# The third mixer's sixteen chunks: a loop of two bodies against code written out, and the mean of the output against a centring matrix

## What is computed

```python
def step(state, inp):                     # state: heads x 64 (v) x 64 (k)
    r_t, w_t, k_t, v_t, al_t, be_t = inp
    sa = jnp.einsum("bhvk,bhk->bhv", state, al_t)
    state = (state * w_t[:, :, None, :] + sa[..., None] * be_t[:, :, None, :]
             + v_t[..., None] * k_t[:, :, None, :])
    return state, jnp.einsum("bhvk,bhk->bhv", state, r_t)

_, y = lax.scan(step, state0, xs)
mean = jnp.mean(y, axis=-1, keepdims=True)
var = jnp.mean(jnp.square(y - mean), axis=-1, keepdims=True)
y = ((y - mean) * lax.rsqrt(var + RW_GN_EPS)).reshape(bsz, seq, RW_WIDTH) * ln_w + ln_b
bonus = jnp.sum(r * k * r_k, axis=-1, keepdims=True) * v
y = y + bonus.reshape(bsz, seq, RW_WIDTH)
return (y * jax.nn.silu(g)) @ w_out
```

## Time and profile before

| | us |
|---|---|
| median of 3 runs | 3883.31 |
| lowest and highest of them | 3881.01, 3886.58 |
| the profiled execution | 3878.87 |
| its span, first to last instruction | 3877.1 |
| span of the stage of this change, from the first L1725 to the end of the last chunk | about 590 |

### The profile page before, as it was taken

One profiled execution on the slowest core, in us unless ns is written; L12 is line 12 of the kernel. 1 busy time (PEld: TensorE's weight loads), 2 busy tenths in 40 slices (PEclk: granted clock), 3 DMA queues, 4 the chain that ended last, 5 costly groups with the idle time before them and its releaser, 6 DMA issues. The chain is left out here.

```text
span 3877.1 us, 74722 instructions
## 1 busy us (share of the span) xinstructions
PE 3420.5 (88%) x32138; PEld 2120.4 (55%) x32138; DVE 1853.0 (48%) x2539; ACT 1387.1 (36%) x2002; POOL 693.2 (18%) x422
## 2 busy tenths in 40 slices
PE   6978999969798697989998899978799999888889
PEld 3335766644343244888887466645544466545434
DVE  3654566552424533545554456633352366623352
ACT  3553445432454431333333435532211255512111
POOL 2000000020000001333332033322260133132330
PEclk8989999979899798999999999999999999999999
DMA  5101101031243443111111221010012211020121
GB/s 157 33 21 53 39 27 38 22 109 33 76 98 93 105 117 105 42 60 51 51 60 40 66 73 49 7 53 28 14 55 71 60 38 33 1 64 17 41 76 44
DMA packets 308035, 215.19 MB, mean 56 GB/s; under 512 B 125379, under 2 KB 283918, under 8 KB 305166
## 3 DMA queue, kind: packets, MB, share of 16 engines
q1 hardware_dynamic: 307320, 210.70, 18.1%
q10 hardware_dynamic: 442, 0.37, 0.0%
HBM read 173.26 MB, written 41.98 MB: 56 GB/s over the span
## 5 line engine op out<-in xcount | busy, mean ns | idle before, releaser
L140 PE MATMUL psum<-u,w_hi 128*128 128x512 f16 x2816 | 857.0, 387 | 101.9 <-DVEq L796 32.1
L140 PE MATMUL psum<-u,w_lo 128*128 128x512 f16 x1408 | 542.6, 385 | 0.0
L140 PEld LDWEIGHTS psum<-u,w_hi 128*128 128x128 f16 x2816 | 279.6, 100 | 451.4 <-issue 57.5
L97 POOL TENSOR_TENSOR w_hi<-stage,w_scale 128x1024 f16<-128x1024 f32 x76 | 144.9, 1907 | 1157.3 <-PE psum L2258 414.1
L1061 PE MATMUL psum<-w_hi,merged 128*128 128x512 f16 x768 | 235.9, 389 | 25.0 <-PEq L2790 9.1
L2468 DVE CUSTOM_DVE_ANT_0 probs_att<-psum,bias_att 128x1024 f32<-128x1024 f32 x128 | 156.7, 1225 | 168.2 <-PE psum L2280 167.7
L2258 PE MATMUL psum<-u,w_hi 128*128 128x512 f16 x768 | 231.4, 383 | 6.3 <-PEq L964 6.3
L140 PEld LDWEIGHTS psum<-u,w_lo 128*128 128x128 f16 x1408 | 140.0, 99 | 173.2 <-issue 12.5
L1061 PE MATMUL psum<-held_hi_out,merged 128*128 128x512 f16 x768 | 231.0, 379 | 0.0
L115 DVE SCALAR_TENSOR_TENSOR w_lo<-stage,w_hi 128x1024 f16<-128x1024 f32 x100 | 120.0, 1220 | 135.2 <-ACT w_hi L109 135.0
L101 POOL TENSOR_TENSOR w_lo<-stage,w_hi 128x1024 f16<-128x1024 f32 x76 | 177.3, 2333 | 10.8
(11 more groups left out here) (441 smaller groups left out, 6815.4 us busy)
## 6 DMA issues: line engine op xcount, KB each, us to landing
stage<-w_in SPq DMA_DIRECT2D x72, 512.0 KB, 3.8
X<-rwkv_chunks SPq DMA_DIRECT2D x16, 1792.0 KB, 7.6
stage<-ab_w_in SPq DMA_DIRECT2D x48, 512.0 KB, 5.1
rwkv_chunks<-work_rp SPq DMA_DIRECT2D x44, 512.0 KB, 5.6
stage<-rw_w_in SPq DMA_DIRECT2D x32, 512.0 KB, 5.0
stage<-w_out SPq DMA_DIRECT2D x24, 512.0 KB, 5.6
X<-x SPq DMA_DIRECT2D x16, 512.0 KB, 10.9
stage<-ab_w_out SPq DMA_DIRECT2D x16, 512.0 KB, 5.3
```

The lines of the kernel that those rows point to most:

```text
L97: pool.tensor_tensor(K.w_hi[:, slot, :], K.stage[:, slot, :], scale, ALU.mult).then_inc(K.w_half[slot], 1)
L140: last = pe.matmul(K.psum[:, bank, :], w[:, k, :], u[:, k, cols], start=(k == 0 and n == 0), stop=(k == KT - 1 and n == 2))
```

## The change

Two things are done in `rwkv_chunks`. The loop is gone: `chunk_steps` calls the body for each chunk from -1 to 15 with a Python number, so all engines get the 17 bodies one behind the other, and all waits are for constants. `held` is gone too: each of its waits is put on the next instruction, and nothing adds to `seen`. SP's loads are written out in the same way, with the four waits that they had.

And the mean of the output is gone: DVE makes `centre`, the identity less a 64th of `pair_ones`, once ahead of the chunks, and v is turned by a 64x64 block of `centre` where it was turned by the identity. The matmul of the mean on TensorE and the subtraction on DVE are dropped; ACT's square waits for its own copy of the output by a drain, where it waited for `centred`.

```diff
+        centre = sb("centre", [P, P])
-        def held(eng, semaphore, value):
-
-            eng.wait_ge(semaphore, value)
-            eng.sem_inc(seen, 1)
-        def program(eng, body):
-
-            body(-1, 1, True, False, True)
-            body(0, 0, True, True, True)
-            with eng.Fori(0, (RW_N - 4) // 2) as i:
-                body(i * 2 + 1, 1, True, True, True)
-                body(i * 2 + 2, 0, True, True, True)
-            body(RW_N - 3, 1, True, True, True)
-            body(RW_N - 2, 0, True, True, False)
-            body(RW_N - 1, 1, False, True, False)
+        def chunk_steps(body):
+
+            for ch in range(-1, RW_N):
+                body(ch, ch % 2, ch + 1 < RW_N, ch >= 0, ch + 2 < RW_N)
...
-                    sp.dma_start(raw[:, p], A["scratch"][bass.ds(ch, 1)].rearrange("c p a j t -> p (c a) j t")
+                    sp.dma_start(raw[:, p], A["scratch"][ch]
                                  ).then_inc(raw_in[p], 16)
                 load(0, 0)
                 load(1, 1)
-                with sp.Fori(0, (RW_N - 2) // 2) as i:
-                    for p in range(2):
-                        sp.wait_ge(ar_ready, i * 2 + (p + 1))
-                        sp.wait_ge(bk_ready, i * 2 + (p + 1))
-                        sp.wait_ge(turned["v"], i * 2 + (p + 1))
-                        sp.wait_ge(gate_ready, i * 2 + (p + 1))
-                        load(i * 2 + (p + 2), p)
+                for ch in range(2, RW_N):
+                    sp.wait_ge(ar_ready, ch - 1)
+                    sp.wait_ge(bk_ready, ch - 1)
+                    sp.wait_ge(turned["v"], ch - 1)
+                    sp.wait_ge(gate_ready, ch - 1)
+                    load(ch, ch % 2)
...
-                    held(pe, ar_ready, c + 1)
-                    held(pe, bk_ready, c + 1)
+                    pe.wait_ge(ar_ready, c + 1)
+                    pe.wait_ge(bk_ready, c + 1)
...
-                            last = pe.matmul(bank(TURN[n])[hp, j], x[hp, j, :], K.ident[hp, hp], start=True, stop=True)
+                            last = pe.matmul(bank(TURN[n])[hp, j], x[hp, j, :], (centre if n == "v" else K.ident)[hp, hp],
+                                             start=True, stop=True)
...
-                def mean(ch):
-                    held(pe, o_ready, ch + 1)
-                    pe.matmul(K.psum[:, MEAN, :], K.pair_ones[:, :], flat(O[:, :, :]), start=True,
-                              stop=True).then_inc(mean_done, 1)
...
-                        held(pe, bv_ready, c + 1)
+                        pe.wait_ge(bv_ready, c + 1)
+                        if c == 0:
+                            pe.wait_ge(centre_ready, 1)
                         turn(c, "v", raw[:, q, V_])
...
-                        held(pe, taken["v"], c + 1)
-                    if finish:
-                        mean(ch)
+                        pe.wait_ge(taken["v"], c + 1)
...
                 def squares(ch):
-                    act.wait_ge(centred, ch + 1)
+                    act.drain()
                     act.activation(sq[:, :, :], O[:, :, :], ACT.Square).then_inc(sq_ready, 1)
...
+                dve.scalar_tensor_tensor(centre[:, :], K.pair_ones[:, :], -1.0 / RW_C, K.ident[:, :],
+                                         ALU.mult, ALU.add).then_inc(centre_ready, 1)
                 dve.sem_inc(h_ready, 1)
...
-                def centre(ch):
-                    dve.wait_ge(mean_done, ch + 1)
-                    dve.scalar_tensor_tensor(flat(O[:, :, :]), K.psum[:, MEAN, :], -1.0 / RW_C,
-                                             flat(O[:, :, :]), ALU.mult, ALU.add).then_inc(centred, 1)
...
-                        held(dve, z_done, c * P_STEPS + (2 * lv + g + 1))
+                        dve.wait_ge(z_done, c * P_STEPS + (2 * lv + g + 1))
```

More of the change, by code:

```diff
@@ L1726, in first_products @@
                     last.then_inc(ab_done, 1)
-                    if after(c):
-                        held(pe, taken["k"], c)
+                    if c > 0:
+                        pe.wait_ge(taken["k"], c)
                     for g in range(2):
@@ L1733, in first_products @@
                     last.then_inc(n_done, 1)
-                    if after(c):
-                        held(pe, t_ready, c * T_STEPS)
+                    if c > 0:
+                        pe.wait_ge(t_ready, c * T_STEPS)
                     for g in range(2):
@@ L1741, in bonus @@
                 def bonus(c, q):
-                    if after(c, 1):
-                        held(pe, rs_ready, c - 1)
+                    if c > 1:
+                        pe.wait_ge(rs_ready, c - 1)
                     pe.matmul(K.psum[:, BONUS, :], K.pair_ones[:, :], flat(bon[:, q]), start=True,
@@ L1780, in right_sides @@
                 def right_sides(ch, p):
-                    held(pe, h_ready, ch + 1)
-                    held(pe, taken["v"], ch + 1)
-                    held(pe, ak_ready, ch + 1)
+                    pe.wait_ge(h_ready, ch + 1)
+                    pe.wait_ge(taken["v"], ch + 1)
+                    pe.wait_ge(ak_ready, ch + 1)
                     for g in range(2):
@@ L1791, in solutions @@
                 def solutions(ch, p):
[L1792 to L1795, removed]
+                    pe.wait_ge(t_ready, ch * T_STEPS + T_STEPS)
+                    if ch > 0:
+                        pe.wait_ge(o_ready, ch)
+                    pe.wait_ge(rhs_ready, ch + 1)
                     for g in range(2):
@@ L1801, in state @@
                 def state(ch, p):
-                    held(pe, u_ready, ch + 1)
-                    held(pe, taken["k"], ch + 1)
+                    pe.wait_ge(u_ready, ch + 1)
+                    pe.wait_ge(taken["k"], ch + 1)
                     for g in range(2):
@@ L1848, in body @@
                         turn(c, "b", bt[:, q])
-                        held(pe, bv_ready, c + 1)
+                        pe.wait_ge(bv_ready, c + 1)
+                        if c == 0:
+                            pe.wait_ge(centre_ready, 1)
                         turn(c, "v", raw[:, q, V_])
                         y_step(c, q, 1)
-                        held(pe, taken["b"], c + 1)
+                        pe.wait_ge(taken["b"], c + 1)
                         turn(c, "k", kt[:, q])
@@ L1867, in body @@
                         z_step(c, q, 4)
-                program(pe, body)
+                chunk_steps(body)
             @block.scalar
@@ L1875, in exponentials @@
                 def exponentials(n, p):
-                    if after(n):
+                    if n > 0:
                         act.wait_ge(ar_ready, n)
@@ L1924, in body @@
                         take_y(c, 0)
-                    if finish and after(ch):
+                    if finish and ch > 0:
                         high_part(ch - 1)
@@ L1949, in _ @@
                 act.wait_ge(t_init, 1)
-                program(act, body)
+                chunk_steps(body)
                 high_part(RW_N - 1)
@@ L2002, in body @@
                         if finish:
-                            held(pool, u_done, ch + 1)
+                            pool.wait_ge(u_done, ch + 1)
                         start_t(p)
@@ L2008, in _ @@
                 prepare(0, 0)
-                program(pool, body)
+                chunk_steps(body)
                 output(RW_N - 1, 1)
@@ L2036, in at_rt @@
                     dve.wait_ge(e3_ready, n + 1)
-                    if after(n, 1):
+                    if n > 1:
                         dve.wait_ge(o_done, n - 1)
@@ L2124, in body @@
                         grow(c, q, 2)
-                    if finish:
-                        centre(ch)
                     if inverse:
@@ L2137, in _ @@
                 at_rt(0, 0)
-                program(dve, body)
+                chunk_steps(body)
                 normed(RW_N - 1)
```

31 lines of the change are left out of this document (14 added, 17 removed).

## The result

The changed kernel takes 3815.99 us (median of 4 runs, 3813.86 to 3820.15) where the kernel before takes 3882.16: a ratio of 0.983, 95% interval 0.9813 to 0.9847. I had forecast 3836.0 and a range of 3817 to 3853: the direction is right, the size is not, 66 us gained for 47 forecast, and the median lies 1 us under the range.

A forecast was written before the change was run, and what follows sets the result against it. The prediction took the stage to be bound by TensorE's own queue. Its terms, -33.9 - 8.4 - 1.8 - 3.2 = -47.3 us, taken from the median 3883.31, gave 3836.0 us, range 3817 to 3853.

The forecast's parts named there:

- The loops: Bodies 1 to 12 written out: five jump pauses and slow clock go, fetch stalls stay, 34.0 us a body; -33.9 us.
- The waits: `held` instructions ride on the next operation; only two places a body, at L1760, are bare; -3.2 us, bounds 0 and -10.
- Most lie under a full queue and cost nothing: Claim that most `held` instructions cost no time, leaving two bare places a body at 0.1 us each.
- The mean: Two matmuls fewer on TensorE, 0.8 us a body, 0.2 where a fetch stall follows: -8.4 us; last body -1.8 us.
- rival A: Stage of the chunks: loop gain comes, the rest is swallowed by fetch stalls and exponentials; -35.7 us, 3847.6; chance 0.21.
- The last body: Body 15, mean through centring to square, all bare: 1.86 us go, 0.1 returns for the drain; -1.8 us.
- What was costed at nothing: Turning v by another 64x64 block at L1750: same 218 ns as its other uses, so nil.
- The signs that I named: No L1725 issue wait but the first, clock 1.00, loaded bodies 32 to 33.5 us, L1750 unchanged, L1772/L1776 stalls 0 to 2.
- Rival B: Stage of the chunks: fewer instructions per body let blocks keep ahead, so stalls go too; -62.3 us, 3821.0; chance 0.14.
- Rival D: Block fetch beside 14 loads starves TensorE and the clock falls; 28 us slower, 3911; chance 0.03.
- The sum: All terms in the stage of the chunks together: -47.3 us, bounds -34 and -73.

The follow-up runs named there:

- small loads: Changed kernel, but from chunk 2 on each load brings one of seven arrays (256 KB for 1792): 3809.92 us; the same with held kept: 3824.66 us.
- the add ahead of the wait: Kernels with held kept, its add to `seen` put before its wait: 3814.98 us with pieced, spread loads (held on TensorE alone), 3834.91 us with whole loads (all three engines).
- paced ones: Changed kernel with each raw load cut into seven arrays of 256 KB, issued one by one along the body: 3811.53 us, ratio 0.9819.

## Why the prediction was right or wrong

**The loops** (forecast -33.9, bounds -29.3 to -45.3): the ratio gives -29, the stage -26.6. Mechanism as forecast: five pauses and the slow clock behind them gone, the fetch stalls kept. The size is a little off (4.9 us by the ratio, 7.3 by the stage) since I took the body at 34.0 from the two bodies outside the loop or at its end, and the twelve take 34.75.

**The waits** (forecast -3.2, bounds 0 to -10): this is the step that failed. Taking held away is worth 26 us with the mean kept and 34 to 38 us with the centring, and that although the change leaves 15 waiting instructions a body on TensorE. "Most lie under a full queue and cost nothing" stands in the prediction without a row of its own. In bodies without a stall it is nearly true: beside small loads 0.5 us a body came back where I had 0.2. What I did not ask is what a waiting instruction does to the fetching of the instructions behind it. The runs with the add ahead of the wait show that it is for the larger part the waiting: as many instructions, 490 of 794 no longer waiting, 17 of 21 us back. And the transfers show where it acts: with held the next block begins to move 0.7 us later in the middle value, and the late ones 1.3 to 1.6 us later. That the sequencer reads on across a wait that a product's own instruction carries, and not across one that stands alone, is the reading that fits all this; the trace has no record of the reading itself.

**The mean** (forecast -8.4 and -1.8): its own working held within its bounds, the size did not. I took 0.8 us a body and bounded it at 0.5; it is 0.55, and the limit is the one named, ACT's exponentials in front of the copy of Y. In body(13) of the changed kernel the copies follow them at once, and TensorE waits:

```profile
2008.88 0.20 ACT L1864 ACTIVATE ee_rc<-u 128x8 f32<-128x8 f32 x1
2008.99 0.62 ACT L1889 COPY u<-psum 128x256 f32<-128x256 f32 x2
...
2009.48 0.68 PE L1757 MATMUL psum<-u,T_rc 64*64 64x64 f32 x16 [0.44 <-ACT u L1889]
```

That stalls take it back was rival A; they take all of it beside held (ratio 0.9997 alone, and nothing again with the loops out), and part of it in the changed kernel, where the centring is worth 7 to 11 us by the ratios, with intervals that overlap, and nothing by the stage. The last body, from ACT's copy of O (L1910) to the square:

```profile
2053.95 0.58 ACT L1910 COPY O_rc<-psum 128x512 f32<-128x512 f32 x1 [2.80 <-PE psum L1801]
2054.61 0.63 ACT L1869 ACTIVATE sq_rc<-O_rc 128x512 f32<-128x512 f32 x1
```

The drain costs under 0.1 us; the mean and centring that stood from 2109.58 to 2111.44 before are gone, as forecast.

**What was costed at nothing** held: the turn of v by `centre` takes 218 ns (before: 218).

```profile
L1734 PE MATMUL psum<-centre_rc,X x512: 218/218/218, 1536.5 to 2032.7; 64*64 64x64 f32 x171
```

**The signs that I named**: no wait at the old jumps and L1750's time unchanged came true; bodies of 32 to 33.5 us did, but for two of 35.0 and 35.7; stalls of 0 to 2 us did, but for two of 2.2 and 2.8; a clock of 1.00 nearly did (0.99; it was 0.5 for 3.4 us at the end of each of these two stalls). Rival B had about the measured time, 3821, for a reason that is wrong: the stalls did not go, they grew from 11.1 to 19.4 us. Rival D points at the right place, the block fetch beside the loads, and these two stalls with the slow clock behind them are small cases of what it priced; there are two in one profile and six falls of the clock in the other.

**The sum** over one profile would have been close (stage -53.2 and -46.8 for -47.3), and that is luck. Taken apart by the stages of the runs, the first is -26.6 for the loops, -27.2 for the waits and +0.6 for the mean, where the forecast had -33.9, -3.2 and -10.2: the waits' price, sized at an eighth, made up for the other two. The medians moved by more because the first profile of before was 3 us under its median and those of the changed kernel 4 and 5 us over theirs. The range left out the bound of an unknown cost that I had put at 10; it should have been three to four times that.

## What to carry to other kernels

That its queue is full does not make a wait free where it stands in an instruction of its own on TensorE: in code of many small matmuls, put it on the operation that needs it. Where TensorE's instruction blocks share the DMA engines with long loads, cut the loads and issue the pieces along the stage; look at the "issue" waits for it. And price a saving on TensorE only after asking whether it is instructions that it will run out of next.

## What the runs showed of the hardware that I had not expected

- An instruction on TensorE that only waits for a semaphore costs far more than its 51 ns where it comes 50 times in a body of 32 us: 34 to 38 us over 16 bodies beside whole loads (there on DVE and POOL too, which had 2 us of it beside paced ones), 21 us beside paced ones, and 5 us beside paced ones if the instructions are there but most of them do not wait.
- TensorE's instructions come in blocks of 16 KB, one for 256 of them, and all 101 of its stalls of over 0.3 us in written-out code stand at the end of a block and end 1.2 to 1.6 us after the next has landed.
- A jump back in TensorE's queue costs 3.2 to 3.8 us of nothing, also with next to no other data moving (2% of the DMA engines' time behind it), and then 3.4 to 6.8 us at a granted clock of 0.5.
- Beside a load of 1792 KB a block of 16 KB of instructions can come so late that TensorE stands 2.8 us; beside the same bytes in pieces of 256 KB, spread over the body, it stood 0.5 us at most. Beside the long loads the block begins to move late and does not move slowly: up to 4.8 us after TensorE has reached the block before it, for 1.8 beside small loads, while its own transfer takes 1.5 us at most.
- Removing 1.05 us of matmuls from TensorE's queue in each of 15 bodies (centring alone) changed nothing, and the stalls grew by 10.5 us.
